# Down projection of a ConvFFN on one core: eight block products replaced by seven, with sums of weight and activation quarters

## What is computed

```python
mixed = (gate_a * y_a + gate_b * y_b) @ w_out
x = x + mixed
hf = rmsnorm(x, norm_ffn_g)
g_pre = causal_dwconv(hf @ ffn_w_gate, ffn_conv_w, ffn_conv_b)
ff = (gelu(g_pre) * (hf @ ffn_w_up)) @ ffn_w_down    # (1024 x 2816) @ (2816 x 1024)
x = x + ff
```

## Time and profile before

| | |
|---|---|
| time, median of 3 runs | 1811.03 us (1804.33 to 1813.93) |
| the profiled execution | 1807.07 us, of which the span of instructions is 1805.3 us |
| mean granted TensorE clock | 0.992 of full |
| matmuls in the span | 8448 |
| down projection, first matmul to the end of the span | 1549.17 to 1805.3 us |

### The profile page before, as it was taken

The page is one execution under the profiler, slowest core; times in us unless marked ns, Lnnn a source line. Parts: engine busy times, 40 slices in busy tenths (PEclk is TensorE's granted clock), DMA queues, the critical chain, the costliest instruction groups (busy, mean ns, idle before and its releaser), DMA issues.

```text
span 1805.3 us, 23423 instructions
## 1 busy us (share of the span) xinstructions
PE 1755.5 (97%) x8448; PEld 1403.1 (78%) x8448; DVE 983.3 (54%) x1482; ACT 573.4 (32%) x1105; POOL 810.6 (45%) x589
## 2 busy tenths in 40 slices
PE   8999999999999988999999999999999999999997
PEld 6777777777777766888888888788888888888786
DVE  6453544565364465443313324788878878534634
ACT  6653454455255521111412223533333333000000
POOL 7544454644444276661227633454554554222221
PEclk9999999999999989999999999999999999999999
DMA  4111311321231134445212344322322322445211
GB/s 176 36 42 43 106 55 42 107 60 42 79 82 48 37 106 130 112 119 164 88 47 94 105 144 171 114 97 70 98 76 70 102 73 93 162 141 186 88 52 47
DMA packets 70529, 167.01 MB, mean 93 GB/s; under 512 B 14432, under 2 KB 31968, under 8 KB 70448
## 3 DMA queue, kind: packets, MB, share of 16 engines
q1 hardware_dynamic: 58192, 154.27, 26.8%
q10 hardware_dynamic: 11792, 10.04, 2.0%
q0 software_dynamic: 464, 1.62, 0.2%
HBM read 132.13 MB, written 32.59 MB: 91 GB/s over the span
## 4 chain that ended last, share of the span: by engine, by line
PE 83%; DVE 6%; DMA 4%; POOL 2%; issue 2%; ACT 2%; SPq 0%; DVEq 0%; POOLq 0%; ACTq 0%
PE bank L964 13%; PE bank L966 13%; PE bank L965 13%; PE bank L1317 7%; PE bank L1319 7%; PE bank L1318 7%; PE bank L1375 4%; PE bank L1377 4%; PE bank L1376 4%; DMA ab<-wgt_scr 2%; PE bank L1099 2%; PE bank L1110 1%; DVE sp L1887 1%; PE bank L1083 1%; DMA raw<-in_wblocks 1%
## 5 line engine op out<-in xcount | busy, mean ns | idle before, releaser
L964 PE MATMUL bank<-hhi,whi 128*128 128x512 f32 x1024 | 420.2, 410 | 10.8 <-POOL wlo L687 3.7
L966 PE MATMUL bank<-hhi,wlo 128*128 128x512 f32 x1024 | 407.0, 398 | 0.0
L965 PE MATMUL bank<-hlo,whi 128*128 128x512 f32 x1024 | 406.6, 397 | 0.0
L687 POOL TENSOR_TENSOR wlo<-raw,whi 128x1024 fp32r<-128x1024 f32 (+1 forms) x84 | 197.1, 2346 | 410.4 <-DVE whi L1711 408.8
L964 PEld LDWEIGHTS bank<-hhi,whi 128*128 128x128 f32 x1024 | 194.7, 190 | 59.0 <-issue 7.1
L966 PEld LDWEIGHTS bank<-hhi,wlo 128*128 128x128 f32 x1024 | 194.5, 190 | 45.8
L965 PEld LDWEIGHTS bank<-hlo,whi 128*128 128x128 f32 x1024 | 195.1, 191 | 40.0 <-issue 0.2
L1496 ACT ACTIVATE sp<-sp,sd 128x128 f32<-128x128 f32 (+1 forms) x192 | 84.2, 440 | 115.9 <-DVE sd L1891 115.7
L937 POOL TENSOR_TENSOR plo<-st,phi 128x512 fp32r<-128x512 f32 x60 | 79.5, 1328 | 58.7 <-ACT phi L1623 57.5
L2167 DVE CAST fhi<-ff 128x1024 fp32r (+1 forms) x44 | 31.4, 715 | 125.5 <-PE bank L1377 125.5
L1711 DVE CAST whi<-raw 128x1024 fp32r<-128x1024 f32 (+1 forms) x84 | 67.5, 804 | 51.9 <-DMA raw<-in_wblocks 41.5
(11 more groups left out here) (300 smaller groups left out, 3796.0 us busy)
## 6 DMA issues: line engine op xcount, KB each, us to landing
raw<-in_wblocks SPq DMA_DIRECT2D x98, 512.0 KB, 3.7
pair<-in_wblocks SPq DMA_DIRECT2D x40, 512.0 KB, 4.8
ff_scr<-ffo SPq DMA_DIRECT2D x22, 512.0 KB, 5.9
ff<-ff_scr SPq DMA_DIRECT2D x22, 512.0 KB, 4.0
ab<-wgt_scr SPq DMA_DIRECT2D x16, 512.0 KB, 5.9
rt<-rt_scr SPq DMA_DIRECT2D x8, 516.0 KB, 6.7
x<-in_xT SPq DMA_DIRECT2D x8, 512.0 KB, 8.5
zb_scr<-zb SPq DMA_DIRECT2D x8, 512.0 KB, 3.5
```

What stands on the lines that cost most here:

```text
L687: pool.tensor_tensor(wlo[par][:, 0:cols], raw[par][:, 0:cols], whi[par][:, 0:cols].bitcast(F32), ALU.subtract).then_inc(lo_done, 1)
L964: nc.tensor.matmul(ps, a, x, start=start and k == k_list[0], stop=False)
L965: nc.tensor.matmul(ps, a, y, start=False, stop=False)
L966: last = nc.tensor.matmul(ps, b, x, start=False, stop=stop and k == k_list[-1])
```

## The change

**Down projection.** Both matrices are cut into 2x2 quarters: the weights by rows (chunks 0 to 10 and 11 to 21) and by output features, the activations by the same chunks and by token halves. Seven products of 128x512 tiles over 11 chunks each are made in the order `M_1, M_2, M_6, M_7, M_5, M_4, M_3`. One chunk of one product is a step t = 0 to 76, of 4 output tiles and 12 matmuls: 77 x 12 = 924. Every operand tile of a step is 128x512 and lies in a ring of four (`RING`): `dw_raw`, `dwhi`, `dwlo` for the weights and `dahi`, `dalo` for the activations. Per step ACT makes two casts (`down_act_hi`, `down_weight_hi`), DVE one subtraction (`down_act_lo`), POOL one (`dwlo`). TensorE's step t needs both `dw_lo` and `da_lo` at t+1; ACT's casts of step t wait until step t-4 was multiplied.

**Activation sums.** They are made in place in `ff`, three steps ahead (`D_AHEAD`): for `M_6` two on DVE per chunk, for `M_5` and `M_4` one on POOL per chunk. SP loads `ff` in halves, along with the weights of a step.

**Weight sums.** They are made once, in the gate and value-and-gate blocks. For each of 11 pairs of chunks ACT issues two loads (`load_rows`), POOL makes four operations in a chain (`weight_sums`), and ACT issues two stores to `wsum_scr` (`store_sums`).

**Ends.** Products are combined in `s17`, `s_2` and the output tiles at fixed steps (`at`); SP stores 16 tiles of 128x512. The last two steps are done tile by tile.

The diff, cut to its core; the numbers of the next rows are of the new file.

```diff
+NK = NF // 2
+STEPS = 7 * NK
+RING = 4
+D_AHEAD = 3
+M_1, M_2, M_6, M_7, M_5, M_4, M_3 = range(7)
...
+            dw_raw = sb("dw_raw", [P, RING, HT])
+            osb = sb("osb", [P, 8, HT])
...
+            dwhi = sb("dwhi", [P, RING, HT], F32R)
+            x1a = sb("x1a", [P, 4, T])
+            s17 = sb("s17", [P, 4, HT])
+            dwlo = sb("dwlo", [P, RING, HT], F32R)
+            x1b = sb("x1b", [P, 4, T])
+            s_2 = sb("s_2", [P, 4, HT])
+            dahi = sb("dahi", [P, RING, HT], F32R)
+            dalo = sb("dalo", [P, RING, HT], F32R)
...
+        def down_weight(t):
+            q, c = divmod(t, NK)
+            if q in (M_1, M_2, M_4):
+                rows = wblocks[116 + c + (NK if q != M_1 else 0)]
+            else:
+                rows = wsum_scr[0 if q in (M_6, M_7) else 1, c]
+            return half(rows, 1 if q in (M_4, M_7, M_5) else 0)
+        def b_part(c, k, h):
+            return half(ff[:, c + NK * k, :], h)
+        def down_act(t):
+            q, c = divmod(t, NK)
+            return b_part(c, *{M_1: (0, 0), M_2: (1, 0), M_6: (0, 0), M_7: (0, 1), M_5: (0, 1), M_4: (1, 0), M_3: (1, 1)}[q])
+        def final_tile(n):
+            m = n % 4
+            x1q, h, q = ((x1a, 0, M_2), (x1b, 1, M_5), (x1b, 0, M_4), (x1a, 1, M_3))[n // 4]
+            return q, m, h, half(x1q[:, m, :], h), osb[:, n % 8, :]
...
+            def load_dw(t):
+                if t >= RING:
+                    sp_.wait_ge(dw_lo, t - RING + 1)
+                sp_.dma_start(dw_raw[:, t % RING, :], down_weight(t)).then_inc(dw_in[t % RING], 16)
...
+            extra = {}
+            for g, h, rows, t0 in ((4, 0, range(15, 22), 8), (5, 1, range(11, 15), 12),
+                                   (6, 1, (4, 15, 5, 16, 6, 17, 7, 18, 8, 19, 9, 20, 10, 21), 16)):
+                for i, f in enumerate(rows):
+                    extra.setdefault(t0 + (i // 2 if g == 4 else i), []).append((load_ff, g, [f], h))
+            for g, t0, step in ((0, 23, 3), (1, 46, 2), (2, 65, 2), (3, 60, 1)):
+                for m in range(4):
+                    extra.setdefault(t0 + step * m, []).append((load_x1r, g, m))
+            for n in range(8):
+                extra.setdefault(34 + 3 * n if n < 4 else 68 + 2 * (n - 4), []).append((store_out, n))
+            for t in range(RING + 3, STEPS):
+                load_dw(t)
+                for f, *args in extra.get(t, ()):
+                    f(*args)
...
+            def weight_sums(c):
+                pool.wait_ge(ws_in[c % 2], 32 * (c // 2 + 1))
+                a11, a21, a12, a22 = (half(ws[c % 2][:, k, :], d) for k in range(2) for d in range(2))
+                link(tt(a22, a21, a22, ALU.add))
+                link(tt(a21, a11, a21, ALU.subtract))
+                link(tt(a11, a22, a11, ALU.subtract))
+                tt(a12, a12, a11, ALU.subtract).then_inc(ws_done, 1)
...
                 lo(B_E2 + m + 1, (m + 1) % 2)
+                if m:
+                    weight_sums(m - 1)
             for m in range(KC):
                 lo(B_VG + m + 1, (m + 1) % 2)
+                if KC - 1 + m < NK:
+                    weight_sums(KC - 1 + m)
...
+            def down_act_sum(t):
+                q, c = divmod(t, NK)
+                b11, b12, b21, b22 = (b_part(c, k, h) for k in range(2) for h in range(2))
+                if q == M_5:
+                    pool.wait_ge(da_sum, c + 1)
+                    pool.wait_ge(da_lo, NK * M_7 + c + 1)
+                    pool.tensor_tensor(b12, b22, b11, ALU.subtract).then_inc(da_sum, 1)
+                elif q == M_4:
+                    pool.tensor_tensor(b21, b21, b11, ALU.subtract).then_inc(da_sum, 1)
+            for t in range(STEPS):
+                if t + D_AHEAD < STEPS:
+                    down_act_sum(t + D_AHEAD)
+                pool.wait_ge(dw_hi, t + 1)
+                pool.tensor_tensor(dwlo[:, t % RING, :], dw_raw[:, t % RING, :], dwhi[:, t % RING, :].bitcast(F32),
+                                   ALU.subtract).then_inc(dw_lo, 1)
...
+            def down_free(q, m):
+                if q == M_1 and m == 1:
+                    pe.wait_ge(copied, NU)
+                elif q == M_1 and m == 2:
+                    pe.wait_ge(cdone, SUMS * (NU - 1) + N_G0)
+                elif q == M_1 and m == 3:
+                    pe.wait_ge(cdone, SUMS * (NU - 1) + N_U2)
+                elif q == M_2 and m == 0:
+                    pe.wait_ge(ff_done, 2 * NF + 4)
+                elif q == M_6:
+                    pe.wait_ge(down_snap, m + 1)
+                elif q > M_6:
+                    pe.wait_ge(down_read, 4 * (q - M_7) + m + 1)
+            def down_tile_mm(t, m):
+                q, c = divmod(t, NK)
+                r, ps = slice(m * P, (m + 1) * P), dbank(q, m)
+                if c == 0:
+                    down_free(q, m)
+                a, b, x, y = dwhi[:, t % RING, r], dwlo[:, t % RING, r], dahi[:, t % RING, :], dalo[:, t % RING, :]
+                nc.tensor.matmul(ps, a, x, start=c == 0, stop=False)
+                nc.tensor.matmul(ps, a, y, start=False, stop=False)
+                last = nc.tensor.matmul(ps, b, x, start=False, stop=c == NK - 1)
+                if c == NK - 1 and m < 3:
+                    last.then_inc(down_tile, 1)
+                return last
+            def operands(t):
+                pe.wait_ge(dw_lo, t + 1)
+                pe.wait_ge(da_lo, t + 1)
+            for t in range(STEPS - 2):
+                operands(t)
+                for m in range(4):
+                    last = down_tile_mm(t, m)
+                last.then_inc(down_used, 1)
+            for t in (STEPS - 2, STEPS - 1):
+                operands(t)
+            for m in range(4):
+                for t in (STEPS - 2, STEPS - 1):
+                    last = down_tile_mm(t, m)
+            last.then_inc(down_used, 2)
...
+            def load_rows(c):
+                if c >= 2:
+                    act.wait_ge(ws_out[c % 2], 32 * (c // 2))
+                for k in range(2):
+                    act.dma_start(ws[c % 2][:, k, :], wblocks[116 + NK * k + c]).then_inc(ws_in[c % 2], 16)
+            def store_sums(c):
+                act.wait_ge(ws_done, c + 1)
+                for k in range(2):
+                    act.dma_start(wsum_scr[k, c], ws[c % 2][:, k, :]).then_inc(ws_out[c % 2], 16)
...
                 for h in range(2):
                     act.wait_ge(gpre, 2 * KC + 2 * m + h + 1)
                     act.activation(half(zt[:, m, :], h), half(zt[:, m, :], h), ACT.Sigmoid).then_inc(sga_done, 1)
+                if m == 0:
+                    act.wait_ge(state_done, HP)
+                    act.wait_ge(m_in, 16 * CH * HP)
+                else:
+                    store_sums(m - 1)
+                load_rows(m)
...
+            def down_weight_hi(t):
+                act.wait_ge(dw_in[t % RING], 16 * (t // RING + 2))
+                if t >= RING:
+                    act.wait_ge(down_used, t - RING + 1)
+                act.activation(dwhi[:, t % RING, :], dw_raw[:, t % RING, :], ACT.Copy).then_inc(dw_hi, 1)
+            def down_act_hi(t):
+                q, c = divmod(t, NK)
+                arrival = {(M_1, 0): (0, 4), (M_1, 4): (1, 4), (M_1, 8): (2, 3), (M_2, 0): (3, 4), (M_2, 4): (4, 7)}.get((q, c))
+                if arrival:
+                    act.wait_ge(ff_in[arrival[0]], ff_in0[arrival[0]] + 16 * arrival[1])
+                if q in (M_6, M_5, M_4):
+                    act.wait_ge(da_sum, {M_6: 0, M_5: NK, M_4: 2 * NK}[q] + c + 1)
+                if t >= RING:
+                    act.wait_ge(down_used, t - RING + 1)
+                act.activation(dahi[:, t % RING, :], down_act(t), ACT.Copy).then_inc(da_hi, 1)
...
+                if last:
+                    for t in range(RING):
+                        down_act_hi(t)
+                    act.wait_ge(prod, SLOTS * u + I_S2)
+                    for t in range(RING):
+                        down_weight_hi(t)
...
+            for t in range(RING, STEPS):
+                down_act_hi(t)
+                down_weight_hi(t)
+                if 0 <= t - RING - NK < 4:
+                    snap(t - RING - NK)
...
+            def down_act_sum(t):
+                q, c = divmod(t, NK)
+                b11, b12, b22 = b_part(c, 0, 0), b_part(c, 0, 1), b_part(c, 1, 1)
+                if q == M_6:
+                    if c in (0, 4):
+                        dve.wait_ge(ff_in[5 + c // 4], ff_in0[5 + c // 4] + 16 * (4, 14)[c // 4])
+                    link(TT(b12, b22, b12, ALU.subtract))
+                    TT(b11, b11, b12, ALU.add).then_inc(da_sum, 1)
...
+            def finish_tile(n):
+                q, m, h, x, tile = final_tile(n)
+                product_in(q, m)
+                if n % 4 == 0:
+                    dve.wait_ge(x1r_in[n // 4], 16 + 64)
+                if n == 8:
+                    dve.wait_ge(out_done, 16 * 8)
+                if n == 0:
+                    dve.wait_ge(down_snap, 4)
```

(25 more changed lines are left out.)

212 lines of the change are left out of this document (83 added, 129 removed).

## The result

| kernel | median | ratio to before | 95% interval |
|---|---|---|---|
| before | 1808.11 us (4 runs) | | |
| after | 1831.54 us (1829.74 to 1832.85, 4 runs) | 1.0126 | 1.0093 to 1.0160 |

A forecast was written before the change was run, and what follows sets the result against it. PE bounds the kernel, busy with matmuls 1755.5 of 1805.3 us. A 35.3 us loss in the gate blocks less a 23.0 us gain in the down stage made it 12.3 us slower, 1823.3 us; range 1804 to 1842.

The forecast's parts named there:

- A: Down stage, step 23: PE waits 6.1 us for DVE, whose sum for step 26 needs the last group's 14 loads.
- B: Down stage, step 27: PE waits 5.2 us for DVE, whose first output tile needs four late-loaded residual tiles.
- The down projection: what is saved: Down stage: 924 matmuls instead of 1056 and a shorter end, less waits; 233.1 us instead of 256.1, a gain of 23.0.
- the clock: Down stage: matmuls run at a lower granted clock after each of two PE pauses; 1.8 us each, 3.6 together.
- the tail: End of the down stage, from last matmul through last operations and store: 4.7 us instead of 9.7.
- POOL in `M_5` and `M_4`: Down stage, 22 steps: POOL's two operations, one slowed by DVE, take 3.2 us per 2.72 us step; PE waits 4 us.
- First sum: Gate blocks, block 3: POOL waits for ACT's first loads, then sums before its subtraction; PE waits 12.9 us.
- The turn: Gate blocks: two stores, two loads (7.0 us) and POOL's sum (5.5) in one chain, 12.5 us against PE's 11.15.
- Value-and-gate blocks: Value-and-gate blocks: POOL adds its own four operations (5.7 us), then three rounds of 13.6 us; block 5's weights ready at 1027.3.
- much slower: Gate blocks: SP's own 512 KB load shares the transfers, 13.9 us per round, loss 46, time 1834; chance 0.20.
- the upper bound of the loss: Gate blocks: with 8.7 us for transfers, 14.2 us per round, block 5 ready at 1039.8, a loss of 48.

## Why the prediction was right, and which term was mis-sized

The time lay in the range and on the right side, 8 us above the forecast. That flatters it: before came out 2.9 us lower beside after than in the runs that the forecast started from, and the difference, 12.3 us forecast, was 23.4. Its signs came: a wait of 10.5 us near 880, then four of 1.4 to 4.1 in the next blocks, 4.7 and 4.9 at 978 and 996, and both A and B. The spans differ by 25.6: a loss of 47.4 in the gate blocks (by POOL's last z operation) for 35.3, and a gain of 21.7 in the down stage for 23.0. By its own steps:

- **The down projection: what is saved.** 23.0 us forecast; 234.4 us measured for 233.1, a gain of 21.7 in the trace and 22.5 by the run without sums. The terms are near: matmuls 0.2267 apart; *waits A and B* 6.1 + 5.2 and *the clock* 3.6 are 14.9, where the window of after lacks 67 of 198 matmuls, 15.2 us, and moving the loads made the stage 13.4 us shorter (11.8 by the medians); the tail is 3.9 (1826.61 + 0.39 to 1830.9) for 4.7.
- ***POOL in `M_5` and `M_4`*,** 4 us (0 to 6.5): 4.1 to 5.5 by moving its sums to DVE. The size is luck, since two steps behind it were off. POOL's rows, at one place:

```profile
1736.22 1.74 POOL L1040 TENSOR_TENSOR ff<-ff 128x512 f32<-128x512 f32 x1
1737.92 1.30 POOL L1048 TENSOR_TENSOR dwlo<-dw_raw,dwhi 128x512 fp32r<-128x512 f32 x1
1739.18 1.75 POOL L1040 TENSOR_TENSOR ff<-ff 128x512 f32<-128x512 f32 x1
```

  A step is 2.96 us, not 3.2: one of the two operations is slowed, by 0.45, and not by a whole operation of DVE. Over all 22 steps (1715.53 to 1781.12) it is 2.98 on average, which puts POOL 5.8 us behind PE's pace and not 10.5. With the 5.5 us by which I let POOL be late unfelt, 0.3 would have been left; PE felt over 4. So POOL's step was priced too high and its slack too large, and the slack that it really had is not shown. By the rule of the Trainium skill (SBUF — State Buffer, "Who interferes with whom") I had estimated a step of 3.2; the direction agrees, and the size is less here.
- ***First sum.*** 12.9 us forecast, 10.5 measured. ACT's issue of the loads stands at 876.17, its table load at 877.18 and its sigmoids at 878.48, two of which come ahead of the loads in the program. I had put the issue behind those two, at 880.3. The opening says that an engine takes its instructions strictly in program order, a DMA issue included; for the start of ACT's issues against its computing these rows show otherwise. The sums then took 6.6 us (881.30 to 887.92), not 5.5, beside VectorE's work.
- ***The turn.*** This is the step that was mis-sized: 12.5 us forecast, 14.35 measured, six times, 19.2 us of loss for 8.1. Its chain was right, and the run that only swaps two lines shows it. Its transfers were not 7.0 but 9.0 us. I had added one first landing of 2.6 and 1.4 us for each further transfer, as if stores and loads on one queue were one stream. The runs give the parts: without stores the loads take 10.80 - 5.7 = 5.1 us from one sum to the next, and the first pair of all, with nothing else under way, took 5.1 too (876.17 to 881.30). I had allowed 1.4 + 1.4 and 0.2 of waking up for them, 3.0. The stores make 3.9 of the 9.0, and I had given them 2.6 + 1.4 = 4.0. So the whole error is the landing of the two loads, for which the earlier trace rows had the row: `pair`, 4.8 us.
- **Value-and-gate blocks.** One turn of +7.1 (7.0 forecast) and three of +3.05 (2.45): GpSimd's sum there meets VectorE's work, and single operations take 2.02 us instead of 1.29. The profile puts PE's wait there down to `DVE t`; in the kernel DVE's product waits for `z_done`, POOL's signal.
- **The rival "much slower"** had the time nearly right (turn 13.9, loss 46, 1834). That is mostly luck. Its mechanism is true in kind: SyncE's load lands in 5.3 us instead of 3.5, so queues do share, as the Trainium skill has it (DMA: Bandwidth & Descriptors, "Issuing engines are not separate DMA queues"). But the turn hardly felt it: half of SyncE's bytes were worth 0.38 us of it in one profile and nothing by the medians, and a pair of loads took 5.1 us with SyncE's load beside it and without. What made the turn 1.85 us longer than forecast is the landing of two loads, which I had priced from a stream of eight.
- **A slip.** In the upper bound of the loss block 5 stands at 1039.8; its own steps give 990.3 + 8.1 + 3 x 13.6 = 1039.2, a loss of 47. Nothing hangs on it.

## What to carry to other kernels

Work that is put into an engine's idle time costs nothing only if its data is there when its turn in the queue comes: an in-order engine that waits for a load holds back all that stands behind it. Issue the next load before you wait for the result of the last; here this was the order of two calls and 24 us. And price a small chain of transfers by a row of a pair that nothing preceded, not by the rate inside a long stream: the pair took 5.1 us here, and by the stream it was 3.0.
